# Gate, up and most of down as two-level block products, in sets of four output tiles

## What is computed

```
g  = xn @ w_gate                      # (1056 tokens) x 1024 @ 1024 x 2816
gb = concatenate([conv_state, g])     # two earlier tokens per sequence
gc = conv_b + sum(conv_w[j] * gb[j:j+t] for j in range(3))
y  = (silu(gc) * (xn @ w_up)) @ w_down          # 2816 x 1024
yp = yp + y ;  also returned: the last two rows of gb
```

## Time and profile before

| what | value |
|---|---|
| median of 3 runs | 2527.1 us |
| runs | 2522.76 to 2531.39 us |
| span of the profiled execution | 2534.1 us |
| its gate/up stage | 1683.6 to 2244.9 us |
| its down stage | 2244.9 to 2534.1 us |
| mean granted PE clock | 0.968 |

### The profile page before, as it was taken

One profiled execution on the slowest core, in us unless ns is written; L12 is line 12 of the kernel. 1 busy time (PEld: TensorE's weight loads), 2 busy tenths in 40 slices (PEclk: granted clock), 3 DMA queues, 4 the chain that ended last, 5 costly groups with the idle time before them and its releaser, 6 DMA issues. The chain is left out here.

```text
span 2534.1 us, 32744 instructions
## 1 busy us (share of the span) xinstructions
PE 2334.3 (92%) x12445; PEld 1567.3 (62%) x12445; DVE 1080.7 (43%) x2405; ACT 738.3 (29%) x2025; POOL 690.6 (27%) x731
## 2 busy tenths in 40 slices
PE   7999998886898899888799899989999999999999
PEld 5644444553455565555544345458888888888887
DVE  5479987771355633343313113344333433370001
ACT  3342244653455455544401014211111111100000
POOL 1031122113565455567500010022221222101110
PEclk9999998997999999998999899999999999999999
DMA  4211101004798788866540203101111111122221
GB/s 142 72 61 70 43 1 42 1 1 159 290 340 315 253 311 320 299 212 187 159 151 1 83 27 140 67 36 51 35 51 34 51 35 51 34 78 69 72 65 39
DMA packets 148609, 281.76 MB, mean 111 GB/s; under 512 B 14486, under 2 KB 83782, under 8 KB 148454
## 3 DMA queue, kind: packets, MB, share of 16 engines
q0 software_dynamic: 49408, 176.19, 20.3%
q1 hardware_dynamic: 80758, 90.50, 10.8%
q10 hardware_dynamic: 18288, 12.98, 1.7%
HBM read 261.68 MB, written 17.94 MB: 110 GB/s over the span
## 5 line engine op out<-in xcount | busy, mean ns | idle before, releaser
L629 PE MATMUL PS<-region 128*128 128x512 f32 (+5 forms) x864 | 330.8, 538 | 1.9 <-DMA region<-w_in 1.9
L2680 PE MATMUL PS<-region,ffn_w 128*128 128x264 f32 x1408 | 323.3, 388 | 1.6 <-PEq L2131 1.6
L2680 PEld LDWEIGHTS PS<-region,ffn_w 128*128 128x128 f32 x1408 | 269.4, 191 | 48.6 <-issue 2.0
L629 PEld LDWEIGHTS PS<-region 128*128 128x128 f32 (+1 forms) x864 | 154.6, 183 | 162.5 <-issue 142.1
L1912 ACT COPY region<-PS 128x512 f32<-128x512 f32 x352 | 193.6, 593 | 186.2 <-PE PS L1791 89.4
L2680 PE MATMUL PS<-region,side 128*128 128x264 f32 x1056 | 243.3, 387 | 1.6 <-POOL side L2637 1.6
L2680 PEld LDWEIGHTS PS<-region,side 128*128 128x128 f32 x1056 | 198.9, 190 | 35.0 <-POOL side L2637 1.7
L909 DVE TENSOR_SCALAR_CACHE_REDUCE mask<-score,cand 128x384 bf16<-128x384 f32 (+2 forms) x198 | 180.7, 943 | 4.2
L1791 PE MATMUL PS<-ident_f,region 128*128 128x128 f32 x1024 | 141.9, 281 | 23.8 <-ACT region L1912 21.6
L1660 POOL DMA_INDIRECT region<-cache_b_k,gather_b x128 | 121.2, 947 | 134.2 <-PE PS L1791 107.7
L1791 PEld LDWEIGHTS PS<-ident_f,region 128*128 128x128 f32 x1024 | 114.4, 144 | 49.4 <-issue 42.7
(11 more groups left out here) (436 smaller groups left out, 3986.2 us busy)
## 6 DMA issues: line engine op xcount, KB each, us to landing
ffn_w<-w_gate SPq DMA_DIRECT2D x11, 1024.0 KB, 5.3
ffn_w<-w_up SPq DMA_DIRECT2D x11, 1024.0 KB, 5.5
region<-w_in SPq DMA_DIRECT2D x4, 2048.0 KB, 8.1
ffn_w<-w_down ACTq DMA_DIRECT2D x7, 704.0 KB, 5.4
region<-x_prompt ACTq DMA_DIRECT2D x8, 512.0 KB, 7.3
region<-x_prompt SPq DMA_DIRECT2D x8, 512.0 KB, 10.6
mem_keys<-cache_mem_k SPq DMA_DIRECT2D x8, 512.0 KB, 4.1
mem_values<-cache_mem_v SPq DMA_DIRECT2D x8, 512.0 KB, 7.9
```

The lines of the kernel that those rows point to most:

```text
L629: last = nc.tensor.matmul(M.PS[0:n, s % 3, 0:chunks[j].width], XT[:, c, t * P:t * P + n], w[j % 2][:, c, 0:chunks[j].width], start=(c == 0 ...
L2680: last = nc.tensor.matmul(M.PS[:, bank, 0:TW], left[:, c, :], right[:, c, :], start=begin and c == 0, stop=(c == KH - 1), skip_group_check ...
```

## The change

`ffn_stage` and `down_stage` are replaced by one `ffn_stage` that is driven by a plan, `FfnPlan`. Nothing before the feed-forward part changes, other than that its first weights are loaded as four blocks of 512 KB.

- **Two levels.** The work is 15 sets: gate and up of four output tiles each (`G`, `U`), one mixed set `M` with gate and up of tiles 16 and 17, gate and up of tiles 18 to 21, and four sets of down (`a` for k-tiles 0 to 7 and `b` for k-tiles 8 to 15, two each). Each set is a 4 x 8 x (4 pieces of 264 tokens) product, done as 7 outer products (steps), each of them again 7 inner products of two matmuls: 49 for 64. The last 6 k-tiles of down are 8 closing steps of one level, 7 products of 3 matmuls.
- **Order on PE.** In step s PE executes P1 of s, P4 of s-1, P2 of s, P3 of s-1, then P6, P5 and P7 of s. P3 of s-1 waits for DVE's sum ("q", s-1, 22), and successive steps use two sets of PSUM banks.
- **Order on DVE.** `vector_steps(s)` writes it out: "q" are sums of inner products (one input from PSUM), "u" and "g" are sums over outer products (`block_sum`; both inputs in SBUF but for part 21), "h" (`join`) multiplies up results into `H` or adds to the output, "X" and "x" are the outer and inner sums of the moving side (2112 and 528 columns), "v" is the convolution of one tile (four steps in succession at the end of a gate set and in the next set), "y" the addition of the residual.
- **Order on POOL.** Four sums of 256 columns a step into a ring of three, and four of 512 columns a set (`weight_steps`). The sums of step s may start when P3 of step s-3 is done.
- **Gated tiles.** `H` has four tiles only. SP stores each finished tile to the new DRAM tensor `h_scratch` and loads it back, in halves of tokens, as moving side of down.
- **Output.** Down's results are added up in SBUF (`yT`) and turned in the closing steps, 72 transposes of 128 columns.

The diff, cut to its core:

```diff
-def ffn_stage(nc, io, M, K, XT, H):
...
+class FfnPlan:
...
+    PLACE = {1: (0, 0), 4: (1, 1), 5: (1, 0), 6: (0, 1)}
+    HALF = {11: 0, 12: 1, 21: 2, 22: 3}
+    ROLES = ("A11", "A12", "A21", "A22", "S1", "S2", "S4")
+    LEFT = ("A11", "A12", "S2", "A21", "S1", "A22", "S4")
...
+        self.sets = [(kind, q) for q in range(4) for kind in "GU"] + [("M", 4), ("G", 5), ("U", 5)]
+        self.sets += [(kind, q) for kind in "ab" for q in range(2)]
+        self.outer = 7 * len(self.sets)
+        self.ends = [(q, i, n) for q in range(2) for i in range(2) for n in range(2)]
...
+        self.products = []
+        for s in range(self.total + 1):
+            self.products.append([(t, o) for t, o in (("P1", s), ("P4", s - 1), ("P2", s), ("P3", s - 1), ("P6", s),
+                                                      ("P5", s), ("P7", s)) if 0 <= o < self.total])
+        self.mm = {key: x + 1 for x, key in enumerate(itertools.chain(*self.products))}
...
+    def weight_steps(self, n):
+        s = 7 * n
+        sums = lambda k: [("s", s + k, j) for j in (1, 3, 2, 4)]
+        return (sums(0) + sums(1) + [("S", n, 1), ("S", n, 2)] + sums(2) + [("S", n, 3), ("S", n, 4)]
+                + sums(3) + sums(4) + sums(5) + sums(6))
...
+    def vector_steps(self, s):
+        if 0 < s <= self.total:
+            o, k = s - 1, (s - 1) % 7 if s - 1 < self.outer else 7
+            yield ("q", o, 22)
+            if k == 4:
+                yield ("g", o, 21)
+                yield ("g", o, 22)
+            if k:
+                yield ("u", o, 21)
+                yield ("u", o, 22)
+        if 0 <= s < self.total:
+            yield ("q", s, 11)
+        if 0 < s <= self.total:
+            yield ("q", o, 12)
+        if 0 <= s < self.outer and s % 7 == 4:
+            yield ("g", s, 11)
+        if 0 <= s < self.total and (s % 7 or s >= self.outer):
+            yield ("u", s, 11)
+        if 0 < s <= self.total:
+            if k == 4:
+                yield ("g", o, 12)
+            if k:
+                yield ("u", o, 12)
+            if self.kind(o) in "Ub" and k in self.PLACE:
+                for c in (11, 21, 22, 12):
+                    yield ("h", o, c)
+        for first, v in self.first.items():
+            b = s - 7 * first
+            if b == -1:
+                yield ("X", v, 1)
+            if b == 1:
+                yield ("X", v, 2)
+            if b == 2:
+                yield ("X", v, 3)
+            if -1 <= b <= 5:
+                for j in (1, 2, 3, 4):
+                    if b == 1 and j == 3:
+                        yield ("X", v, 4)
+                    yield ("x", v, b + 1, j)
+        if s - self.outer in (-1, 0):
+            for j in (1, 2, 3, 4):
+                yield ("e", s - self.outer + 1, j)
+        for n in self.gates:
+            b = s - 7 * n
+            for at, row in self.conv_order(n):
+                if b == at:
+                    yield ("v", n, row)
+            if b == (9 if self.sets[n][0] == "M" else 11):
+                yield ("w", n)
+            if self.sets[n][0] == "M" and b in (8, 9):
+                yield ("m", n, b - 8)
+        for x, (o, z, part) in enumerate(self.phases):
+            if o == s - 2:
+                yield ("y", x)
...
+    BLOCK = 2 * TW
+    RING = 3
...
+        right = [B11, B21, T2, B12, T1, T4, B22]
...
+        def bank(t, s):
+            return {"P1": A, "P6": A, "P7": A, "P4": A, "P2": D2}.get(t, C) + s % 2
...
+                def add(out, a, b, op, after):
+                    if after:
+                        pool.wait_ge(made, made_at[after])
+                    nc.gpsimd.tensor_tensor(out, a, b, op).then_inc(made, 1)
+
+                def sums(left, out, key):
+
+                    y11, y12, y21, y22 = left
+                    add(out[0], y21, y22, ALU.add, None)
+                    add(out[2], y11, y21, ALU.subtract, None)
+                    add(out[1], out[0], y11, ALU.subtract, key + (1,))
+                    add(out[3], y12, out[1], ALU.subtract, key + (2,))
...
+                        if key[0] == "s" and key[2] == 1:
+                            s, k = key[1], key[1] % 7
+                            role = plan.LEFT[k]
+                            if role in ("A11", "A12", "A22"):
+                                pool.wait_ge(w_in[role], 16 * (n + 1))
+                            else:
+                                pool.wait_ge(made, made_at["S", n, {"S2": 2, "A21": 3, "S1": 1, "S4": 4}[role]])
+                            if s >= RING:
+                                pool.wait_ge(mm, all_done(s - RING))
+                            y = at[role]
+                            sums((part(y, 0, 0, P), part(y, 1, 0, P), part(y, 0, 1, P), part(y, 1, 1, P)),
+                                 [ring[:, s % RING, x] for x in range(4)], ("s", s))
+                        elif key[0] == "S":
+                            if key[2] == 1:
+                                pool.wait_ge(w_in["A21"], 16 * (n + 1))
+                                pool.wait_ge(w_in["A22"], 16 * (n + 1))
+                                if n:
+                                    pool.wait_ge(mm, all_done(7 * (n - 1) + 3))
+                                add(at["S1"], at["A21"], at["A22"], ALU.add, None)
+                            elif key[2] == 2:
+                                if n:
+                                    pool.wait_ge(mm, all_done(7 * (n - 1) + 4))
+                                add(at["S2"], at["S1"], at["A11"], ALU.subtract, ("S", n, 1))
+                            elif key[2] == 3:
+                                add(at["A21"], at["A11"], at["A21"], ALU.subtract, None)
+                            else:
+                                if n:
+                                    pool.wait_ge(mm, all_done(7 * (n - 1) + 5))
...
+                def store_h(n, row):
+                    sp.dma_start(M.h_scr.ap()[plan.tiles(n)[0] + row], H[:, row, :]).then_inc(h_stored[row], 16)
+
+                def load_h(dst, f, tokens, name):
+                    sp.dma_start(dst, h_rows[:, f, tokens]).then_inc(h_in[name], 16)
...
+                    if n in plan.first and v:
+                        load_h(B22, slice(8 * v - 4, 8 * v), second, "B22")
+                    if n and sets[n - 1][0] == "U":
+                        sp.wait_ge(summed, summed_at["h", 7 * n - 1, 12])
+                        for row in (2, 3):
+                            store_h(n - 2, row)
...
+                    if closing:
+                        for r in range(4):
+                            sp.wait_ge(h_stored[r], 16 * (2 * v + 2))
+                        load_h(B11, slice(8 * v, 8 * v + 4), first, "B11")
...
+                def product(t, s):
+                    left, moved = operands(t, s)
+                    begin = t in ("P1", "P2", "P5")
+                    if t == "P1" and s >= 2:
+                        if s - 2 < outer and (s - 2) % 7 == 0:
+                            pe.wait_ge(a_copied, (s - 2) // 7 + 1)
+                        else:
+                            pe.wait_ge(summed, summed_at["u", s - 2, 21])
+                    elif t == "P2" and s >= 2:
+                        pe.wait_ge(summed, summed_at["q", s - 2, 11])
+                    elif t == "P5" and s >= 2:
+                        pe.wait_ge(summed, summed_at["q", s - 2, 12])
+                    elif t == "P3":
+                        pe.wait_ge(summed, summed_at["q", s, 22])
+                    elif t in ("P6", "P7", "P4"):
+                        pe.wait_ge(copied, 3 * s + {"P6": 1, "P7": 2, "P4": 3}[t])
+                    kt = 3 if s >= outer else 2
+                    for c in range(kt):
+                        last = nc.tensor.matmul(M.PS[:, bank(t, s), 0:TW], left[:, c, :], moved[:, c, :],
+                                                start=begin and c == 0, stop=(c == kt - 1), skip_group_check=not begin)
+                    last.then_inc(mm, 1)
...
+                for s in range(total + 1):
+                    for t, o in plan.products[s]:
+                        product(t, o)
...
+                def copy(s, t, c):
+                    x = {11: 0, 12: 1, 22: 2}[c]
+                    act.wait_ge(mm, mm_at[t, s])
+                    if s >= 2:
+                        act.wait_ge(summed, plan.last_use(s - 2, c))
+                    nc.scalar.copy(mine[:, s % 2, x, :], M.PS[:, bank("P1", s), 0:TW]).then_inc(copied, 1)
...
+                def product_sum(s, c):
+                    x = {11: 1, 12: 2, 22: 3}[c]
+                    dve.wait_ge(copied, 3 * s + x)
+                    t = {11: "P2", 12: "P3", 22: "P5"}[c]
+                    dve.wait_ge(mm, mm_at[t, s])
+                    out = own(s, c)
+                    if s < outer and s % 7 == 0:
+                        out = UA[:, HALF[c], :]
+                        if s:
+                            dve.wait_ge(summed, summed_at["u", s - 1, c])
```

(33 more changed lines are left out.)

1080 lines of the change are left out of this document (565 added, 515 removed).

## The result

| | before | after |
|---|---|---|
| median, same chip (4 runs each) | 2528.44 us | 2675.50 us |
| runs | 2522.76 to 2531.39 | 2669.27 to 2676.48 |
| ratio, 95% interval | 1 | 1.0577 (1.0559 to 1.0595) |
| span of the profiled execution | 2534.1 us | 2674.3 us |
| mean granted PE clock | 0.968 | 0.942 |

The changed kernel is 5.8% slower, outside the range of 2470 to 2600 us. The page's first part answers to the earlier trace rows: PE has less to do and a smaller share, DVE is busy 503 us longer and POOL 366.

A forecast was written before the change was run, and what follows sets the result against it. PE was taken as the bound, busy 92% of the span. Stalls and other waits of 124 us, less 95.7 us gained mostly by fewer products, gave +28.5 us on 2527.1: 2556 us, range 2470 to 2600.

The forecast's parts named there:

- port waits: DVE operations with SBUF inputs alternate with POOL's sums, 0.97 us lost per 512 columns: 1.7 us, 3.7 in steps 6 and 0.
- forecast, upper: Stalls if all DVE and POOL sums that can collide do, over the feed-forward steps, start and closing: 144.2 us.
- end of an up set, two steps: Steps with eleven and ten DVE operations, at the end of up sets, stall 0.8, then 0.1 us.
- a moving side (a0): Where the first down half begins, DVE's sums of its new moving side stall PE 22.7 us; 8.5 without port waits.
- The loop itself: P3 waits for DVE's sum behind six products; stall is DVE's own time plus port waits minus 6.04 us, if positive.
- 80% of collisions: Of the 100.6 us between lower and upper stalls, 80% was taken, 80.5 us, giving 124 us of stalls.
- rival D: PE's granted clock falls, at 0.93 in the rewritten stretch, about 30 us more: 2586 us; chance 0.05.
- the gain: Fewer block products on PE, 3276 records against 3696: 93.5 us; with transposes and hand-over 95.7 us.
- the lower bound: With no collisions of DVE and POOL, stalls of 43.6 us less 95.7 gained: -52 us, 2475 us.
- rival C: DVE operations spaced by their full 0.43 us, not 0.35: 24 us more, 2580 us; chance 0.05.
- the wait for POOL's first sums: At the start of the rewritten stretch PE idles 8.1 us for POOL's third sum, for 1.6 before: 6.5 us.
- Rival A: DVE's and POOL's sums pass each other in convolution and moving-side steps, so the kernel is faster: typical 2490 us; chance 0.38.

The follow-up runs named there:

- e4: Changed kernel with 622 extra 128-column products keeping PE busy ahead of P3's waits in the steps that stall; 2653.5 us.
- e2: Changed kernel with only POOL's outer weight sums (1024 columns each) reduced to 4 columns of each tile, outputs incomplete; 2567.1 us.
- e1: Changed kernel with nearly all of POOL's weight sums left out, only 4 columns of each tile made, outputs incomplete; 2487.7 us.
- e8: Changed kernel with each outer weight sum on POOL made as four instructions of 256 columns in the same place; 2604.2 us.
- e16: Changed kernel with POOL's sums cut short, 16 tiles' first convolution multiplication on ACT, fourth tile's convolution later, later moving-side sums spread earlier; 2529.6 us, 1.0004 of the kernel before.
- e5: Changed kernel with the four outer weight sums of a set placed one by one in other steps, none in steps 6 and 0; 2654.5 us.

## Why the prediction was wrong

**The step that failed is the size of the port waits.** The prediction counted "28 sums of 256 columns and four of 512 per set"; the four have 1024, and took 2.35 us undisturbed (the 23 shortest of 60 records: 2.34 to 2.36) instead of 1.27. Two of them meet a DVE stretch at each boundary of sets, so what it called 3.7 us of port waits is 3.7 + 2 x 1.08 = 5.9. e4, with the clock nearly held, lets the formula be read step by step (us above 6.23, in the step in which PE shows it):

```
stall                                 forecast, upper   with 1024 columns   e4
convolution of step 6 of a gate set        4.1                6.3           6.1
of step 0 of the up set                    3.7                5.9           5.9
of step 1                                  1.7                1.7           1.7
of step 2                                  3.5                3.5           3.7
end of an up set, two steps                0.9                5.0           5.7
a moving side (a0)                        22.7               27.0          29.4
```

The loop itself, six products of cover against DVE's own time and its port waits, was right to some tenths of a microsecond. Two choices in it were not. The 80% of collisions were 100%: the columns fit only at the upper bound. And 512 was a misreading of the diff, in which a set's block is four tiles of 256. With both put right, the forecast's terms come to about 200 us of stalls (five pairs 87, the mixed set 12, five ends of sets 25, the moving sides 68, start and closing 10). e4 has 877.2 - 654.2 - 3.3 (turns of the state) = 220 in the 105 steps, some 7 of them the fill's, where the forecast has 121 (its 124 without the closing).

The forecast missed by 119 us, 147 for 28.5. By estimate from these terms, some 58 of them are the 1024 columns, 20 the share of collisions and 22 or more the clock, which was not in the sum. The rest, some 20, lies mostly in the first set and the down halves, and its cause stays open. e2 measures the long sums as a whole: 108 us hang on them.

**The clock** was not in the sum, only in rival D. The products took 64.9 us more than before, mostly at the lower level, but only 22 us came back in e4, which lifted most of it; D's "about 30" was near, as an addition and not as a rival. The changed kernel's idle time (168 us in the 105 steps) is under the 220 of stalls because PE spent part of its waiting in slow products.

**Point by point.** Right: the gain (3276 records expected and 3276 in the trace, 93.5 us); the lower bound (e1: -43 for -52); nearly no stall from ACT or DMA; the four stalled steps with a convolution, and where the down halves begin; the spacing of operations by 0.35 us (1991.53 to 1991.87), against rival C. At the start the wait for POOL's first sums stands where it was expected, with 6.3 us for 8.1: the 1.8 us of products ahead of it took 3.8 us at the lower clock. Wrong: the two steps at the end of an up set, which were given 0.9 us, stall by 5.7; the 32-column operations were expected near 1.22 and took up to 2.21; closing has 4.0 us idle in its steps for 1.6, and 2.2 us more than before behind the last product for 1.5. Rival A, that the sums pass each other, did not happen by itself; only e8 to e16 forced part of it.

## What to carry to other kernels

Where DVE and GpSimd both read SBUF and DVE is on the path, price each DVE operation with one whole GpSimd instruction, and cut the GpSimd instructions short as long as GpSimd has time for it: that gave 71 and 23 us here, for edits of a few lines, and left GpSimd busy for 87% of the steps. Shorter pieces than 128 columns were not tried. Read operand sizes from the access pattern, not from the name of the block, before pricing a collision. And where an engine idles for a late helper, look at what its clock costs only after asking whether that time is waited for anyway.

## What the runs showed of the hardware

- POOL's float32 sum of two SBUF operands takes 0.45, 0.72, 1.27, 2.35 and 3.17 us for 128, 256, 512, 1024 and 1408 columns. Cut in 128 columns the same work takes a fifth more (711 for 598 us), and the kernel still gains.
- The loss of a short operation doesn't depend on its own length: 32 columns took 2.21 us beside a long sum and 0.25 at the same place beside short ones.
- The collisions are not confined to operations with two SBUF inputs. The convolution's first multiplication, which reads one tile in SBUF, took up to 0.76 us for 32 columns and up to 1.28 for 1024 in the changed kernel; with POOL's sums narrow (e1) it took 0.30 and 0.83 at most.
- Moving long sums away from the steps that stalled (e5) gave 21 us; cutting them where they were gave 71.
- In one session every kernel was some 6% slower (2684 for 2529 us), all of it ahead of the rewritten part, with a lower granted clock in stages that no edit touched (0.87 for 0.94). It isn't shown to be a property of the chip: the record gives the same chip number for e16, where the kernel before took 2530.4 us. Its cause is open.
